# Delta rule: the triangular inverse on four 32-row tiles instead of two 64-row halves

## The reference

```python
def _gated_delta_rule(q, k, v, beta, g):
    ...
    decay = jnp.where(tri, jnp.exp(jnp.where(tri, diff, 0.0)), 0.0)
    kb = k * beta[..., None]
    a_mat = jnp.eye(c, dtype=F32) + jnp.where(strict, jnp.einsum('bhnid,bhnjd->bhnij', kb, k) * decay, 0.0)
    rhs = jnp.concatenate([v * beta[..., None], kb * jnp.exp(gc)[..., None]], -1)
    sol = lax.linalg.triangular_solve(a_mat, rhs, left_side=True, lower=True, unit_diagonal=True)
    ...
    def step(state, inp):
        qd_n, u_n, w_n, attn_n, kd_n, gl_n = inp
        v_new = u_n - jnp.einsum('bhcd,bhde->bhce', w_n, state)
        o_n = jnp.einsum('bhcd,bhde->bhce', qd_n, state) + jnp.einsum('bhij,bhje->bhie', attn_n, v_new)
        state = state * jnp.exp(gl_n)[..., None, None] + jnp.einsum('bhcd,bhce->bhde', kd_n, v_new)
        return state, o_n
```

## Time and profile before

| | us |
|---|---|
| median of three runs | 2808.88 (2799.04 to 2811.01) |
| the profiled execution's own time | 2807.05 |
| its span, first to last instruction | 2805.2 |
| TensorE busy in the span | 2720.0 (97%) |
| the delta rule's eight chunks | 1797 to 2041 |

### The profile page before, as it was taken

The page is one execution under the profiler, slowest core; times in us unless marked ns, Lnnn a source line. Parts: engine busy times, 40 slices in busy tenths (PEclk is TensorE's granted clock), DMA queues, the critical chain, the costliest instruction groups (busy, mean ns, idle before and its releaser), DMA issues. The chain is left out here.

```text
span 2805.2 us, 45291 instructions
## 1 busy us (share of the span) xinstructions
PE 2720.0 (97%) x17613; PEld 2296.6 (82%) x17613; DVE 2109.1 (75%) x3262; ACT 1287.0 (46%) x2294; POOL 342.6 (12%) x273
## 2 busy tenths in 40 slices
PE   9999988989999999999999999899999999999998
PEld 7888877888888888888878887788888888888886
DVE  6644445683889999898889985356648999998978
ACT  5333345752444444433357654566543544444332
POOL 0000065240000000000000001365501000000001
PEclk9999999999999999999999999999999999999999
DMA  4323253425322222293332433532043122224652
GB/s 183 120 105 120 75 184 90 135 57 195 120 84 91 90 76 83 88 351 129 102 120 98 149 100 122 179 122 93 18 158 110 57 91 83 91 75 178 232 191 90
DMA packets 162414, 339.12 MB, mean 121 GB/s; under 512 B 35552, under 2 KB 69536, under 8 KB 151584
## 3 DMA queue, kind: packets, MB, share of 16 engines
q1 hardware_dynamic: 143632, 321.54, 32.6%
q10 hardware_dynamic: 18576, 14.75, 1.8%
HBM read 252.17 MB, written 84.05 MB: 120 GB/s over the span
## 5 line engine op out<-in xcount | busy, mean ns | idle before, releaser
L2284 POOL TENSOR_TENSOR ffn_down_rstd<-ffn_down_rstd,ffn_down_power 128x1 f32<-128x1 f32 x15 | 15.0, 1002 | 1263.3 <-DVE ffn_down_rstd L2220 1263.3
L862 DVE TENSOR_TENSOR even_in_w_lo<-even_in_raw_left,even_in_w_hi 128x512 fp32r<-128x512 f32 x80 | 49.9, 686 | 88.2 <-ACT even_in_w_hi L787 88.2
L745 PE MATMUL even_in_acc<-even_in_w_hi,even_x_hi 128*128 128x512 f32 x256 | 99.6, 389 | 0.0
L746 PE MATMUL even_in_acc<-even_in_w_lo,even_x_hi 128*128 128x512 f32 x256 | 99.6, 389 | 0.0
L747 PE MATMUL even_in_acc<-even_in_w_hi,even_x_lo 128*128 128x512 f32 x256 | 99.6, 389 | 0.0
L3769 DVE SCALAR_TENSOR_TENSOR even_mixed<-even_mixed,odd_qkv_taps 128x1023 f32<-128x1023 f32 (+2 forms) x72 | 92.2, 1281 | 4.9 <-ACT even_mixed L3602 3.2
L3255 DVE CUSTOM_DVE_ANT_0 dil_probs<-dil_bank,dil_mask 128x128 f32<-128x128 f32 (+1 forms) x192 | 56.0, 346 | 38.2 <-PE dil_bank L3165 33.4
L747 PE MATMUL even_in_acc<-even_in_w_hi,even_in_s_lo 128*128 128x512 f32 x192 | 74.7, 389 | 0.0
L745 PE MATMUL even_in_acc<-even_in_w_hi,even_in_s_hi 128*128 128x512 f32 x192 | 74.7, 389 | 0.0
L746 PE MATMUL even_in_acc<-even_in_w_lo,even_in_s_hi 128*128 128x512 f32 x192 | 74.7, 389 | 0.0
L3215 ACT ACTIVATE dil_probs<-dil_probs,dil_neg_peak 128x128 f32<-128x128 f32 (+1 forms) x192 | 70.6, 442 | 4.2 <-DVE dil_neg_peak L3260 4.1
(11 more groups left out here) (839 smaller groups left out, 9259.1 us busy)
## 6 DMA issues: line engine op xcount, KB each, us to landing
ffn_w_raw<-in_ffn_up SPq DMA_DIRECT2D x42, 1024.0 KB, 4.8
even_mixed<-in_ffn_down SPq DMA_DIRECT2D x28, 512.0 KB, 5.0
odd_mixed<-in_ffn_down SPq DMA_DIRECT2D x28, 512.0 KB, 3.9
hp<-even_in_stage SPq DMA_DIRECT2D x13, 1024.0 KB, 4.2
even_out_w_raw<-in_ev_w_out SPq DMA_DIRECT2D x22, 512.0 KB, 3.6
hidden<-even_mixed SPq DMA_DIRECT2D x22, 512.0 KB, 2.6
ffn_w_raw<-in_od_w_qkv SPq DMA_DIRECT2D x11, 1024.0 KB, 5.7
hidden<-odd_mixed SPq DMA_DIRECT2D x22, 512.0 KB, 2.6
```

The source lines that it names most:

```text
L745: pe.matmul(to, hi[:, tok], wh, start=(opens and k == 0), stop=False, skip_group_check=not opens)
L746: pe.matmul(to, hi[:, tok], wl, start=False, stop=False, skip_group_check=not opens)
L862: dve.tensor_tensor(w_lo[:, p % 2, k], source(i)[:, k], f32(w_hi[:, p % 2, k]), ALU.subtract).then_inc(lo_ready, 1)
```

## The change

The 64-row blocks of levels 1 to 5 become 32-row tiles (`SUB`): `xt_sub`, `x_sub` and `t_sub` hold four tiles of 32 rows and 32 columns a head. In levels 1 to 4 all three products of a tile stay on its own rows and columns, so b is read where it stands and `b_across` and `move_blocks` go. Level 5 joins tiles 0 and 1, and 2 and 3, by 32-row corner products: two for t, two for d, and one for e, since of the inverse itself only the lower half is needed for level 6. Level 6 is the same 64-row corner as before, now from `x_blk` (lower half) and `xt`, into which `place_blocks` copies six tiles: two of `x_sub` and four of `xt_sub`. For this `place_blocks` stands ahead of `finish_outputs` on ScalarE, and `scale_values` ahead of `copy_y`. VectorE joins level 5 by three copies a group instead of two subtractions. GpSimd's `start` runs over four tiles instead of two halves. New waits: `products_b` of level 6 on `x_placed`, `products_x` of level 6 on `xt_placed`, `join` of level 5 on `v_done` and `t_done` of the chunk before.

The core of the diff:

```diff
-    r, j = i[:, None] % BLK, np.arange(BLK)[None, :]
+    r, j = i[:, None] % SUB, np.arange(SUB)[None, :]
     first = -((r // 2 == j // 2) & (r < j)).astype(np.float32)
     unit = (r == j).astype(np.float32)
     joins = []
-    for level in range(1, LEVELS):
+    for level in range(1, LEVELS - 1):
...
-        xt_blk = sc.sbuf("xt_blk", [P, 2, H, BLK])
+        xt_sub = sc.sbuf("xt_sub", [P, 2, H, SUB])
+        x_sub = sc.sbuf("x_sub", [P, H, SUB])
+        t_sub = sc.sbuf("t_sub", [P, H, SUB])
...
+        quarters = bank[:].rearrange("p b (e h t) -> p b e h t", h=HG, t=SUB)
+        t_ps, d_ps, e_ps, first_ps = ([quarters[:, b + q, e] for q in range(2)]
+                                      for b, e in ((0, 0), (2, 0), (0, 2), (2, 2)))
+        t_half, last_ps = ([halves[:, q, e] for q in range(2)] for e in range(2))
...
-                        for half, across in halves_across:
-                            mm = pe.matmul(first_ps[q][across, h % HG], xt_blk[half, m % 2, h], ident[half, half], start=True, stop=True)
+                        for r in subs:
+                            mm = pe.matmul(first_ps[q][r, h % HG], xt_sub[r, m % 2, h], ident[r, r], start=True, stop=True)
...
-                    pe.wait_ge(b_moved, 4 * n + 2 * q + 2)
                     if n > 0:
                         pe.wait_ge(tm_done, LV * n)
                 else:
                     pe.wait_ge(x_joined, JV * n + 2 * (l - 2) + q + 1)
+                if l == LEVELS:
+                    pe.wait_ge(x_placed, 2 * n + 2)
                 pe.sem_inc(tiles_seen, 1)
-                b = b_across[:, n % 2]
+                b = b_mat[:, n % 2]
                 for h in in_group(q):
                     if l == LEVELS:
-                        mm = pe.matmul(t_ps[q][high, h % HG], b[high, h, high], x_blk[high, h], start=True, stop=True)
+                        mm = pe.matmul(t_half[q][high, h % HG], b[low, h, high], x_blk[low, h], start=True, stop=True)
+                    elif l == LEVELS - 1:
+                        for i, j in (subs[0:2], subs[2:4]):
+                            mm = pe.matmul(t_ps[q][j, h % HG], b[i, h, j], x_sub[i, h], start=True, stop=True)
                     else:
-                        for half, across in halves_across:
-                            mm = pe.matmul(t_ps[q][half, h % HG], b[across, h, half], x_blk[across, h], start=True, stop=True)
+                        for r in subs:
+                            mm = pe.matmul(t_ps[q][r, h % HG], b[r, h, r], x_sub[r, h], start=True, stop=True)
...
+                if l == LEVELS:
+                    pe.wait_ge(xt_placed, 4 * n + 4)
                 pe.sem_inc(tiles_seen, 1)
                 for h in in_group(q):
                     if l == LEVELS:
-                        mm = pe.matmul(last_ps[q][low, h % HG], t_m[high, h], xt_blk[high, s, h], start=True, stop=True)
+                        mm = pe.matmul(last_ps[q][low, h % HG], t_m[high, h], xt[high, h, high], start=True, stop=True)
+                    elif l == LEVELS - 1:
+                        for i, j in (subs[0:2], subs[2:4]):
+                            pe.matmul(d_ps[q][i, h % HG], t_sub[j, h], xt_sub[j, s, h], start=True, stop=True)
+                        mm = pe.matmul(e_ps[q][subs[1], h % HG], xt_sub[subs[1], s, h], t_sub[subs[1], h], start=True, stop=True)
                     else:
-                        for half in (low, high):
-                            pe.matmul(d_ps[q][half, h % HG], t_m[half, h], xt_blk[half, s, h], start=True, stop=True)
-                        for half, across in halves_across:
-                            mm = pe.matmul(e_ps[q][across, h % HG], xt_blk[half, s, h], t_m[half, h], start=True, stop=True)
+                        for r in subs:
+                            pe.matmul(d_ps[q][r, h % HG], t_sub[r, h], xt_sub[r, s, h], start=True, stop=True)
+                        for r in subs:
+                            mm = pe.matmul(e_ps[q][r, h % HG], xt_sub[r, s, h], t_sub[r, h], start=True, stop=True)
...
-            def move_blocks(m):
-                if m > 1:
-                    act.wait_ge(t_done, LV * (m - 1))
-                for q in range(2):
-                    act.wait_ge(b_done, 2 * m + q + 1)
-                    act.copy(group(b_across[high, m % 2], q), group(b_mat[low, m % 2], q)).then_inc(b_moved, 1)
-                    act.copy(group(b_across[low, m % 2], q)[:, :, high], group(b_mat[high, m % 2], q)[:, :, high]).then_inc(b_moved, 1)
-
             def place_blocks(n):
-                act.wait_ge(xt_done, LV * n + LV - 2)
+                if n == 0:
+                    act.wait_ge(zeroed, 2)
+                act.wait_ge(x_joined, JV * n + JV - 2)
+                if n > 0:
+                    act.wait_ge(t_done, LV * n)
+                for r in subs[0:2]:
+                    act.copy(x_blk[r, :, r], x_sub[r]).then_inc(x_placed, 1)
+                act.wait_ge(xt_done, LV * n + LV - 4)
                 if n > 0:
                     act.wait_ge(v_done, 2 * n)
-                for half in (low, high):
-                    act.copy(xt[half, :, half], xt_blk[half, n % 2]).then_inc(xt_placed, 1)
+                for r in subs:
+                    act.copy(xt[r, :, r], xt_sub[r, n % 2]).then_inc(xt_placed, 1)
...
                     decays(n + 1)
                     fade_state(n)
+                    scale_values(n + 1)
                 if n > 0:
                     copy_y(n - 1)
                 if more:
-                    scale_values(n + 1)
                     scale_rows(n + 1)
+                place_blocks(n)
                 if n > 0:
                     finish_outputs(n - 1)
-                if more:
-                    move_blocks(n + 1)
-                place_blocks(n)
                 if more:
                     copy_x(n + 1)
...
-                    dve.tensor_tensor(group(t_m, q), t_ps[q], joins[:, l - 1].unsqueeze(1).broadcast_to([P, HG, BLK]),
+                    dve.tensor_tensor(group(t_sub, q), t_ps[q], joins[:, l - 1].unsqueeze(1).broadcast_to([P, HG, SUB]),
                                       ALU.mult).then_inc(tm_done, 1)
 
             def join(n, l, q):
@@ -4731,9 +4743,16 @@
                     if n > 0:
                         dve.wait_ge(v_done, 2 * n)
                     dve.tensor_copy(group(xt[low, :, high], q), last_ps[q][low]).then_inc(xt_done, 1)
...
+                elif l == LEVELS - 1:
+                    if n > 0:
+                        dve.wait_ge(v_done, 2 * n)
+                        dve.wait_ge(t_done, LV * n)
+                    dve.tensor_copy(group(x_blk[subs[1], :, subs[0]], q), e_ps[q][subs[1]]).then_inc(x_joined, 1)
+                    dve.tensor_copy(group(xt[subs[2], :, subs[3]], q), d_ps[q][subs[2]])
+                    dve.tensor_copy(group(xt[subs[0], :, subs[1]], q), d_ps[q][subs[0]]).then_inc(xt_done, 1)
...
+                for i, r in enumerate(subs):
+                    pool.tensor_tensor(xt_sub[r, s], b_mat[r, s, :, r], first_c[r], ALU.mult).then_inc(first_done, 1)
+                    pool.wait_ge(first_done, 4 * m + i + 1)
+                pool.tensor_tensor(xt_sub[:, s], xt_sub[:, s], unit_c[:], ALU.add).then_inc(start_done, 1)
```

52 lines of the change are left out of this document (24 added, 28 removed).

## The result

The changed kernel takes 2873.49 us (median of 4 runs, 2871.53 to 2879.25) where the kernel before takes 2809.85 on the same chip (4 runs, 2799.04 to 2811.01): 1.0239 times as long, 95% interval 1.0209 to 1.0268. By that ratio it is 67 us slower; 2880 was forecast.

What follows compares the result with a forecast made beforehand. TensorE was taken to be bound by its program's block fetch: 67 blocks at 4.7 us, 315 us against 244, add 71 to 2807, giving 2878, plus 2 for the median: 2880 us, range 2835 to 2940.

Steps and rivals of the forecast that it cites:

- The diagnosis: TensorE's program comes in blocks of 256 instructions, one fetched ahead after the current one is entered; "issue" stops are late blocks.
- The counts: TensorE's program: +1,600 products, four instructions each, +6,400; blocks in the stage 42 to 67, q8 packets 139 to about 164.
- The block's period of 4.7 us: Delta rule: 67 blocks at 4.7 us make 315 us against 244, +71 us; records from stop to stop 4 to 5.5 us.
- The lower bound: Least time for one block, from the stop at 1915.17: 1.2 + 2.2 = 3.4 us.
- The upper: Upper bound for one block: 5.75 us between two stops with idle DMA (share 0.02).
- The sum for levels 1 to 4: TensorE's work per level: 128 + 256 + 32 + 32 instructions in 4.0 us, 2.3 us a block, too fast for the fetch.
- The array's term: TensorE's smaller products save 2.4 us a chunk, 19 us in the stage, hidden as waiting inside the +71 us.
- Rival D: The array itself gets slow: clock stays low, 2975 us, or 32-row tiles don't run side by side, about 2960; chance 0.10.
- The low clock: Some low clock is in the forecast, hidden in block waits: at 1.2 GHz a block of 2.3 us takes 4.6.
- Idle time by "issue": Sign in the changed profile: TensorE idle by "issue" 60 us or more in the stage where it was 10.
- The other engines: Changed steps of VectorE, ScalarE and GpSimd cost nothing while TensorE waits for blocks; GpSimd's start near 3.3 us.
- Rivals B and C: B: blocks come in time, 2790 us, chance 0.07. C: array saving and fetch cost cancel, 2795 to 2807 us, chance 0.05.

Runs made afterwards that it cites:

- m_fetch: The kernel before with 1,280 further 32x32x32 products in one row at the end of the delta rule: 2876.78 us in one run, 70 above before.
- a_wide: The changed kernel with three of each group's four heads streaming 64 columns for 32 in levels 1 to 4, same instructions: 2874.31 us, 1.0241 times before.
- a_full: The changed kernel with heads streaming up to 128 columns for 32 in levels 1 to 4, same instructions: 2868.06 us, 1.0224 times before.
- a_less_e: The changed kernel without the e products of levels 2 to 4, 12 blocks fewer: 2833.66 us, 1.0104 times before.
- b_more: The kernel before with 192 further one-column products a chunk in levels 1 to 4, 24 blocks more: 2879.83 us, 1.0260 times before.
- a_pair: The changed kernel with each head's first product in levels 1 to 4 as two 64-row block-diagonal products for four 32-row ones: 2868.35 us, 1.0230 times before.

## Why the prediction was right, point by point

- **The diagnosis** (stops named "issue" are blocks that come late, one fetched ahead) held in every run, but that a packet can leave shortly before TensorE reaches the border, as at 1899.3. The counts came out to the packet: 164 on q8, 67 in the stage, +6,400 instructions (51,746 for 45,291 with the vector engines' own). That is the part of the forecast that the result rests on. m_fetch shows the fetch by itself; a_wide and a_full show that the array's work isn't what is waited for, a_less_e that taking instructions out brings time back. b_more, meant as the main witness, isn't one, since 47 of its 73 us are its own work in the array.
- **The block's period of 4.7 us** was right as a mean (317/67) and wrong as a picture. I took a single fetch time between 3.4 and 5.75, lengthened by the loads. It is a distance of some 3.6 us between fetches where nothing hinders them (m_fetch), and 23 blocks of 5 to 10 us: 17 that end with hardly a stop, 15 of them partly at half clock, and 6 that end in a stop of over 1 us because the fetch left late. Most of the distances from stop to stop, 3.6 to 4.5 us, are at or under the forecast's "4 to 5.5". The lower bound, 3.4 from one packet, was the fetch after a stop. The upper, 5.75 with idle DMA, was a fetch too, but a late one: it left at 1866.4, 3.1 us after the border, and its block was used at 1869.12, 2.7 us later, behind a stop of 0.79. The forty slices of 1863 to 1867 in the kernel before have it alone:

```profile
GB/s 0 0 0 0 0 0 0 0 0 0 0 0 0 0 0 0 0 0 0 0 0 0 0 0 0 0 0 0 0 0 0 0 0 0 164 0 0 0 0 0
```

  So the middle of the two bounds was a mean of different things, and that it hit 317/67 was luck. It doesn't carry over: for a_pair 3.7 us a block promised 30 us, and it gave 2.5. The sum for levels 1 to 4 also counts too much: a 128-wide group of 1.09 us is 8 records, so 16 instructions and not 32, and the level's 4.0 us are for 416 instructions, 2.5 us a block instead of 2.3. This changes nothing in the conclusion.
- **The array's term** (-2.4 us a chunk; sets of four at 0.032; 0.65 us for a first-product group, 1.16 for a second-product group) measured -2.0, 0.032, 0.68 and 1.28. As said, it is worth nothing while the blocks are late. Rival D's half about tiles that don't run side by side is out.
- **The low clock** was called hidden in the waits for blocks. In the blocks of levels 1 to 4 it is: 3.83 us at 0.50, 3.72 to 3.97 at 1.00. In the blocks of levels 5 and 6 it isn't, and rival D's other half came true there in small, by the two estimates above 14 to 42 us instead of the 95 of its price. It is inside my sum only because the mean of 4.7 was high enough by accident.
- **Idle time by "issue"** of 60 us or more: the view has about 50. From start to start the stops are 60, since a record is drawn 0.2 us long and covers the first part of each. That is 46 more than before; work at half clock takes 47 more, and the array saved 16, which makes 77 for the measured 73.
- **The other engines** cost nothing, as said. VectorE's join takes 0.29 us for 0.42. GpSimd's start of the inverse takes 4 x 0.72 + 0.72 = 3.6 us for the 3.3 estimated, and held TensorE up once, for 1.1:

```profile
L4850 POOL TENSOR_TENSOR gdn_xt_sub<-gdn_b_mat,gdn_first_c 32x256 f32<-32x256 f32 x28 | 20.0, 716 | 30.9 <-DVE gdn_b_mat L4721 29.2
L4852 POOL TENSOR_TENSOR gdn_xt_sub<-gdn_xt_sub,gdn_unit_c 128x256 f32<-128x256 f32 x7 | 5.1, 724 | 0.5
```

- **Rivals B and C** (the blocks come in time; the two cancel) needed 3.1 to 3.6 us a block over the whole stage. 3.6 is what the fetch by itself does in m_fetch, but this stage is not made of such blocks alone.

The Trainium skill, Advanced Engine Details and Errata, section ISA Cache, with its two lines of 256 instructions, agrees with every stop here: none of m_fetch's 20 blocks was there ahead of its time. That shows how far ahead the program is fetched; how many lines there are, no run shows. Of the gain that the Trainium skill's TensorEngine Tiling, Theoretical Speedup, gives for small dimensions, up to two times for 64 and up to four for 32, the array showed a part in the first product (0.68 us for 1.07) and none in the second (1.28 for 1.09), and the program's supply takes the rest away.

## What to carry to other kernels

Before products are cut into smaller ones, count instructions: here a 32-bit product is four, and below some 3.6 us of array work for 256 of them TensorE waits for its program. Compare block by block, not on average: only one block is fetched ahead, so a long one helps its successor at the most. To take instructions out, leave products out or merge them only as far as the weights don't get wider. When instructions are added as a test, measure first what they cost in the array, from the starts of neighbouring groups: here products of one column cost twice what was taken, and that looked like the fetch.
